# The opening of a two-block transformer and recurrence kernel: the first norm's parameters and the first weight unit are loaded in pieces of their own, and the first weight products stand ahead of the low-rank ones

## The chip, the cores and the metric

The kernel runs on one core of one Trainium2 chip. A core has a matrix engine (TensorE, PE in the profile; its weight loads are PEld), a vector engine (VectorE, DVE), an activation engine (ScalarE, ACT), a general engine (GpSimd, POOL), and SyncE (SP), which here only issues DMA transfers. The metric is the time on the device in microseconds, lower is better.

## The reference

The input is one sequence of 256 positions with 1024 features. Two blocks of two layers each follow one another: a gated linear attention mixer, an attention mixer with rotary positions, each followed by a feed-forward network with a short convolution, then a gated recurrence, a short-convolution mixer, and a last norm. All in float32. Only the beginning matters here:

```
h = rmsnorm(x, norm_mix[0])            # x * rsqrt(mean(x*x) + 1e-6) * weight
proj = h @ w_in
q, k, v, g, r = jnp.split(proj, ...)   # q, k: 512 columns, v, g: 1024, r: 32
r_f, r_b = jnp.split(r, 2, axis=-1)    # the low-rank input of the gates
log_decay = log_sigmoid(r_dir @ w_up + b_up) / 16
```

## The kernel before, in words

**Numbers in two parts.** Each float32 operand of a weight product is split into a high part, which the matrix engine reads in its fast format, and a low part, the difference. A product is three: high by high, high by low, and low by high. For the weights ACT makes the high part (`w_hi`) and DVE the low part (`w_lo`). For the normed input the parts are `h_hi` and `h_lo`, which both lie in the buffer `hh`.

**The stream.** All large weights come from one array, `stream`, in units of 128 by 2048 float32 (1 MB), in the order of their use. SP loads unit u into one of three buffers (`raw`). ACT's `split(u)` writes `w_hi` and adds one to the semaphore `hi_split`. DVE's `split(u)` writes `w_lo`, adds one to `lo_split`, and so frees the raw buffer for unit u + 3. Units 0 and 1 are the columns of q.

**The opening.** There is no scheduler and no loop here; each engine runs a list written by hand, and semaphores join the lists. The 256 positions are two tiles (t = 0, 1) of 128 rows. The order of events is as follows.

- SP issues x (two tiles), then all channel parameters `par` (128 by 548), the low-rank weights `wr`, three raw units, and three copies of the gate weights `gup_raw`. `par` and `wr` count on one semaphore, `consts_loaded`.
- ACT squares x and sums it (`sums`, two halves of 512 columns for each tile). POOL makes 1 / root of the mean from it (`rms_of_x`: the lines 436, 443, 445). DVE multiplies x by it in two halves (`normed`, line 994).
- PE transposes the result, tile by tile, in two groups of four (`turn`, line 1678). Before that it runs 29 transposes of a constant (`WARM`, line 1823), whose results nobody reads.
- The norm's weight is multiplied in as the transposed tile is read from PSUM: by DVE for the first four blocks of tile 0 and for all of tile 1 (`front`, line 1000, semaphore `h_front`), by ACT for the other four of tile 0 (`turned0`, line 524, semaphore `h_hi_ready`). DVE then makes `h_lo` in eight steps (`low`, line 1015), the low part of `wr` (line 1097), and the low parts of units 0 and 1 (line 964).
- PE begins with `rank(0, 0)` (8 products of `wr_hi` and `h_hi`, line 1833), then `product(U_Q, ..)` for unit 0 (16 of high by high, 16 of high by low, line 1844), `rank(0, 1)` and `rank(1, 0)`, the 16 of low by high of unit 0, the 48 of unit 1, the gate products (line 1865), and the units of k (`wide`, line 1764).

POOL issues two more loads on its own queue after the two `rms_of_x` steps: `row` (640 KB written) and `rope` (256 KB).

In PE's list the wait `hi_split` >= 1 stands ahead of the first product of unit 0, and the wait for `wr_hi_ready` ahead of the first rank product.

Of the kernel before, what the change touches and what calls it, by code (L numbers as in the profile page):

```python
# [10 lines left out]
D = 1024  # L11
S = 256
T = S // P
KC = D // P
EPS = 1e-6
# [13 lines left out]
UNIT = 2048  # L29
RAW = 3  # L30
# [106 lines left out]
WARM = 29  # L137
N_CONSTS = 2
# [11 lines left out]
SUMS = {"mix0": 0, "gla": 4, "ffn0": 6, "mix1": 10, "ffn1": 14, "lru": 18, "sc": 22, "final": 26}  # L150
# [23 lines left out]
def two_block_kernel(nc, x_in, stream, par_in, row_in, wr_in, gup_in, gatew_in, rope_in, out):  # L174
# [4 lines left out]
    with ctx:  # L179
        def sem(name):  # L180
            return ctx.enter_context(nc.semaphore(name))
# [85 lines left out]
        consts_loaded, gatew_loaded = sem("consts_loaded"), sem("gatew_loaded")  # L267
# [67 lines left out]
        def copies(a):  # L335

            return a[:, :, :].rearrange("p k (c n) -> p k c n", c=COPIES)
# [21 lines left out]
        def _(sp):  # L359
# [8 lines left out]
            sp.dma_start(par[:, :], par_in).then_inc(consts_loaded, 16)  # L368
            sp.dma_start(wr[:, :, :], wr_in.rearrange("p (c n) -> p c n", c=KC)).then_inc(consts_loaded, 16)
            for u in range(RAW):  # L370
                load(u)
# [36 lines left out]
        def _(pool):  # L408
# [24 lines left out]
            def rms_of_x(name):  # L433
                for t in range(T):
                    pool.wait_ge(sumsq, SUMS[name] + 2 * t + 1)
                    part = nc.gpsimd.tensor_scalar(half_mean[:, t:t + 1], stat[:, 2 * t:2 * t + 1], EPS, None, ALU.add)
                    if name in ROOTS:
                        part.then_inc(half_ready, 1)
                        continue
                    own.mark(part)  # L440
                    own.wait()
                    pool.wait_ge(sumsq, SUMS[name] + 2 * t + 2)
                    own.mark(nc.gpsimd.tensor_tensor(mean[:, t:t + 1], stat[:, 2 * t + 1:2 * t + 2], half_mean[:, t:t + 1], ALU.add))
                    own.wait()
                    nc.gpsimd.tensor_tensor(rstd[:, t:t + 1], mean[:, t:t + 1], power[:, t:t + 1], ALU.pow).then_inc(rms_ready, 1)
# [36 lines left out]
        def _(act):  # L482
# [81 lines left out]
            for t in range(T):  # L564
                act.wait_ge(x_loaded[t], 16)
                sums(t, "mix0")
# [3 lines left out]
            turned0("mix0")  # L570
            split(0)
            split(1)

            own.mark(nc.scalar.activation(lam_p[:, :], par[:, C_LAM:C_LAM + LRU_HEADS], ACT.Abs))
# [382 lines left out]
        def _(dve):  # L957
# [128 lines left out]
            for t in range(T):  # L1086
                dve.wait_ge(x_loaded[t], 16)
                for half in range(2):
                    normed("mix0", t, half)
                if t == 0:  # L1090
                    dve.wait_ge(consts_loaded, 16 * N_CONSTS)
                    front("mix0", 0)
            for b in range(2):
# [4 lines left out]
                                    copies(wr_hi).bitcast(f32), ALU.subtract).then_inc(wr_lo_ready, 1)  # L1098
            split(0)
# [24 lines left out]
            evicted(1)  # L1124
            for d in range(2):
                for b in range(2):
                    dve.wait_ge(z_abs, 2 * d + b + 1)
                    for k in range(2):
                        h = 2 * b + k
                        c = C_GB + GLA_HEADS * d + h  # L1130
                        last = nc.vector.tensor_scalar(la[:, d, h, :], z_of(d, h), par[:, c:c + 1], 0.0, ALU.add, ALU.min)
                        own.mark(last) if k == 0 else last.then_inc(z_read, 1)
# [517 lines left out]
        def _(pe):  # L1650
# [175 lines left out]
            pe.wait_ge(wr_hi_ready, 1)  # L1826
# [10 lines left out]
            def product(u, b, a, c):  # L1837

                for kc in range(KC):
                    if (u, c) == (U_Q, 1):  # L1840
                        has_low("mix0", kc)
# [5 lines left out]

            rank(0, 0)
            pe.wait_ge(hi_split, U_Q + 1)
            product(U_Q, GEN["q"] % 4, 0, 0)  # L1850
# [468 lines left out]
```

## Time and profile before

| | us |
|---|---|
| median of 3 runs | 873.67 (872.7 to 874.02) |
| the profiled execution, its own time | 872.12 |
| its span | 870.1 |
| PE busy in the span | 855.0 (98%) |
| DVE busy | 676.7 (78%) |
| ACT busy | 547.6 (63%) |
| POOL busy | 27.2 (3%) |

The span is the time from the first to the last recorded instruction. Around it lie 2.02 us that the profile does not show. The matrix engine is busy nearly all the time. The change is in the first 20 us of the list, and after it everything is issued in the same order as before.

### The profile page before, as it was taken

To read this page: it belongs to the slowest core of one execution; us is meant where nothing else is said; L and a number is where in the kernel's file an instruction comes from. 1 tells how busy PE (TensorE), PEld (TensorE's weight loads), DVE (VectorE), ACT (ScalarE), POOL (GpSimd) and SP (SyncE) were. 2 spreads that over 40 slices of the span, in tenths; PEclk is the share of its full clock that TensorE was granted. 3 is DMA by queue.
4 is the path that set the end of the run, shared out by engine and by line. 5 is a ranking of instruction groups with operands and counts; after the bars stand their busy time and mean duration, and the time that the engine had idled before them with its cause. 6 is when DMAs were issued, how large, how long until landed. Compare 5 with 4: busy or idle time off the path is not lost.

```text
span 870.1 us, 13406 instructions
## 1 busy us (share of the span) xinstructions
PE 855.0 (98%) x4881; PEld 748.3 (86%) x4881; DVE 676.7 (78%) x966; ACT 547.6 (63%) x750; POOL 27.2 (3%) x48
## 2 busy tenths in 40 slices
PE   8999999999999999999999999999999999999996
PEld 8978789888888888889888888989899788888885
DVE  6898767887877798868787886787887877776764
ACT  5855557656656575576666656568998775555533
POOL 2000100000000041010000000000000000000000
PEclk9999999999999999999999999999999999999998
DMA  8553543665555444226656555435364045645511
GB/s 323 194 197 141 194 145 122 221 220 211 193 199 188 145 161 178 98 98 218 242 194 224 192 199 206 145 145 194 128 234 172 0 153 236 240 173 189 207 59 49
DMA packets 22444, 152.81 MB, mean 176 GB/s; under 512 B 2528, under 2 KB 2656, under 8 KB 5120
## 3 DMA queue, kind: packets, MB, share of 16 engines
q1 hardware_dynamic: 22032, 149.71, 47.4%
q0 software_dynamic: 368, 2.49, 0.8%
q8 instruction: 30, 0.49, 0.2%
q14 instruction: 14, 0.11, 0.0%
HBM read 151.14 MB, written 1.05 MB: 175 GB/s over the span
## 4 chain that ended last, share of the span: by engine, by line
PE 83%; DVE 7%; ACT 2%; DMA 1%; issue 1%; POOLq 0%; POOL 0%; SPq 0%; ACTq 0%; DVEq 0%
PE acc L1777 28%; PE ring L1711 24%; PE ring L1715 12%; PE ring L1764 7%; PE acc L1996 3%; DVE w_lo L964 2%; PE ring L1978 1%; PE ring L1726 1%; DMA raw<-in_stream_dram 1%; DVE hh L1028 1%; PE ring L2036 1%; PE ring L2154 1%; ACT w_hi L491 1%; PE acc L1678 1%; PE acc L1791 0%
## 5 line engine op out<-in xcount | busy, mean ns | idle before, releaser
L964 DVE TENSOR_TENSOR w_lo<-raw,w_hi 128x2048 fp32r<-128x2048 f32 (+1 forms) x145 | 318.0, 2197 | 5.7 <-ACT w_hi L491 5.6
L491 ACT ACTIVATE w_hi<-raw 128x2048 fp32r<-128x2048 f32 (+1 forms) x146 | 266.9, 1840 | 53.3 <-DMA raw<-in_stream_dram 50.0
L1711 PE MATMUL ring<-hh,w_hi 128*128 128x512 f32 x944 | 235.7, 392 | 0.8 <-DVE usum L1079 0.8
L1711 PEld LDWEIGHTS ring<-hh,w_hi 128*128 128x128 f32 x944 | 171.4, 189 | 32.8 <-issue 1.0
L1715 PEld LDWEIGHTS ring<-hh,w_lo 128*128 128x128 f32 x944 | 128.8, 190 | 9.2
L1715 PE MATMUL ring<-hh,w_lo 128*128 128x256 f32 x944 | 131.6, 282 | 0.0
L1777 PE MATMUL acc<-w_hi,a_hi 128*128 128x512 f32 x264 | 103.8, 393 | 1.0 <-DVE a_lo L1304 0.9
L1777 PE MATMUL acc<-w_lo,a_hi 128*128 128x512 f32 x264 | 103.1, 391 | 0.0
L1777 PE MATMUL acc<-w_hi,a_lo 128*128 128x512 f32 x264 | 102.7, 389 | 0.0
L1079 DVE TENSOR_TENSOR usum<-ring,usum 128x512 f32<-128x512 f32 x65 | 44.7, 688 | 63.8 <-ACT usum L496 63.6
L1764 PE MATMUL ring<-hh,w_hi 128*128 128x256 f32 x480 | 87.7, 285 | 0.8 <-DVE gg L1543 0.8
L1274 DVE SCALAR_TENSOR_TENSOR cacc<-usum,par,cacc 128x255 f32<-128x255 f32 x168 | 73.8, 480 | 16.1 <-ACT cacc L648 10.9
L1777 PE MATMUL acc<-w_hi,hh 128*128 128x512 f32 x256 | 84.3, 398 | 1.2 <-DVE hh L1000 0.8
L1764 PEld LDWEIGHTS ring<-hh,w_hi 128*128 128x128 f32 x480 | 75.3, 192 | 1.6 <-issue 1.1
L496 ACT ACTIVATE usum<-ring 128x512 f32<-128x512 f32 x65 | 38.1, 587 | 53.8 <-PE ring L1715 52.3
L1764 PE MATMUL ring<-hh,w_lo 128*128 128x256 f32 x240 | 67.9, 283 | 0.0
L1777 PEld LDWEIGHTS acc<-w_hi,a_hi 128*128 128x128 f32 x264 | 49.7, 188 | 11.2 <-DVE a_lo L1304 1.1
L1777 PEld LDWEIGHTS acc<-w_hi,a_lo 128*128 128x128 f32 x264 | 49.6, 188 | 10.6
L1777 PEld LDWEIGHTS acc<-w_hi,hh 128*128 128x128 f32 x256 | 48.1, 188 | 11.6 <-DVE hh L1000 1.0
L1777 PEld LDWEIGHTS acc<-w_lo,a_hi 128*128 128x128 f32 x264 | 49.7, 188 | 9.0
L1777 PE MATMUL acc<-w_lo,hh 128*128 128x512 f32 x128 | 49.9, 390 | 0.0
L648 ACT ACTIVATE cacc<-usum,par 128x256 f32<-128x256 f32 x84 | 45.5, 590 | 6.9 <-DVE usum L1079 6.9
(242 smaller groups left out, 958.0 us busy)
## 6 DMA issues: line engine op xcount, KB each, us to landing
raw<-in_stream_dram SPq DMA_DIRECT2D x134, 1024.0 KB, 4.8
raw<-in_stream_dram SPq DMA_DIRECT2D x12, 512.0 KB, 3.8
gatew<-in_gatew_dram POOLq DMA_DIRECT2D x1, 1536.0 KB, 7.1
x<-in_x_dram SPq DMA_DIRECT2D x2, 512.0 KB, 3.7
out_dram<-xn SPq DMA_DIRECT2D x2, 512.0 KB, 2.6
row<-in_row_dram POOLq DMA_DIRECT2D x1, 640.0 KB, 9.0
gup_raw<-in_gup_dram SPq DMA_DIRECT2D x3, 128.0 KB, 13.6
par<-in_par_dram SPq DMA_DIRECT2D x1, 274.0 KB, 4.5
```

The costliest lines, as they stand in the source:

```text
L491: nc.scalar.activation(w_hi[:, u % RING, 0:n], raw[:, u % RAW, 0:n], ACT.Copy).then_inc(hi_split, 1)
L496: nc.scalar.activation(usum[:, k, :, :], ring[:, 2 * k:2 * k + 2, S:2 * S], ACT.Copy).then_inc(cross_ready, 1)
L648: last = nc.scalar.activation(cacc[:, k, half, :], ring[:, 2, half * S:(half + 1) * S] if alone else usum[:, k, half, :], ACT.Identity, sc ...
L964: nc.vector.tensor_tensor(w_lo[:, u % RING, 0:n], raw[:, u % RAW, 0:n], w_hi[:, u % RING, 0:n].bitcast(f32), ALU.subtract).then_inc(lo_spl ...
L1028: last = nc.vector.scalar_tensor_tensor(out=h_lo[:, kc, part], in0=turned_at(name, t, kc), scalar=par[:, c:c + 1], in1=h_hi[:, kc, part].b ...
L1079: nc.vector.tensor_tensor(usum[:, k, :, :], ring[:, 2 * k:2 * k + 2, 0:S], usum[:, k, :, :], ALU.add).then_inc(summed, 1)
L1274: last = nc.vector.scalar_tensor_tensor(out=cacc[:, k, half, out_at], in0=at, scalar=par[:, bass.ds(c, 1)], in1=cacc[:, k, half, out_at], ...
L1711: nc.tensor.matmul(ring[:, 2 * k + f, :], w_hi[:, u % RING, lo:lo + P], hh[:, kc, :, :], start=kc == 0, stop=False, skip_group_check=True)
L1715: last = nc.tensor.matmul(ring[:, 2 * k + f, 0:S], w_lo[:, u % RING, lo:lo + P], h_hi[:, kc, :], start=False, stop=kc == KC - 1, skip_grou ...
L1764: last = nc.tensor.matmul(ring[:, b, f * S:(f + 1) * S], w_parts[a][:, slot, lo:lo + P], h_parts[c][:, kc, :], start=kc == 0 and n == 0, s ...
L1777: last = nc.tensor.matmul(acc[:, t, half * 512:(half + 1) * 512], lhs(a, kc, t), w_parts[c][:, slot, j * D + half * 512:j * D + (half + 1) ...
L1996: last = nc.tensor.matmul(acc[:, t, half * 512:(half + 1) * 512], of_h(a, kc, t), w_parts[c][:, (U_AQ + n) % RING, j * D + half * 512:j * ...
```

## The change

Five things are done.

1. **Loads.** The eight columns of `par` that hold the first norm's weight come alone (semaphore `gamma_loaded`), directly behind x. Unit 0 follows in two halves of 128 by 1024 (`raw_front` and `raw_loaded[0]`). Then come `wr`, unit 1, the other 540 columns of `par` (`par_loaded`), unit 2 and the gate weights.
2. **Sums.** For the first norm ACT squares a tile in one instruction of 1024 columns, where there were two of 512. POOL makes the mean in one step instead of two. The numbering of the sums (`SUMS`) follows.
3. **ACT's order.** `turned0` comes first, then the high part of unit 0 in two halves (semaphores `hi_front` and `hi_split`), then `wr_hi`, which stood ahead of both, and then unit 1.
4. **PE's order.** The 16 high by high products of unit 0 come ahead of `rank(0, 0)`, with a wait for each half of `w_hi`.
5. **Warm-up.** `WARM` is 27 instead of 29.

```diff
-            sp.dma_start(par[:, :], par_in).then_inc(consts_loaded, 16)
+            sp.dma_start(par[:, 0:KC], par_in[:, 0:KC]).then_inc(gamma_loaded, 16)
+            half = UNIT // 2
+            sp.dma_start(raw[:, 0, 0:half], stream[0, :, 0:half]).then_inc(raw_front, 16)
+            sp.dma_start(raw[:, 0, half:UNIT], stream[0, :, half:UNIT]).then_inc(raw_loaded[0], 16)
             sp.dma_start(wr[:, :, :], wr_in.rearrange("p (c n) -> p c n", c=KC)).then_inc(consts_loaded, 16)
-            for u in range(RAW):
-                load(u)
+            load(1)
+            sp.dma_start(par[:, KC:N_PAR], par_in[:, KC:N_PAR]).then_inc(par_loaded, 16)
+            load(2)
...
                 for t in range(T):
-                    pool.wait_ge(sumsq, SUMS[name] + 2 * t + 1)
-                    part = nc.gpsimd.tensor_scalar(half_mean[:, t:t + 1], stat[:, 2 * t:2 * t + 1], EPS, None, ALU.add)
...
-                    own.mark(part)
-                    own.wait()
-                    pool.wait_ge(sumsq, SUMS[name] + 2 * t + 2)
-                    own.mark(nc.gpsimd.tensor_tensor(mean[:, t:t + 1], stat[:, 2 * t + 1:2 * t + 2], half_mean[:, t:t + 1], ALU.add))
+                    pool.wait_ge(sumsq, SUMS[name] + t + 1)
+                    own.mark(nc.gpsimd.tensor_scalar(mean[:, t:t + 1], stat[:, 2 * t + 1:2 * t + 2], EPS, None, ALU.add))
                     own.wait()
...
             for t in range(T):
                 act.wait_ge(x_loaded[t], 16)
-                sums(t, "mix0")
+                nc.scalar.activation(xn[:, t, :], x[:, t, :], ACT.Square, scale=D ** -0.5,
+                                     accum_out=stat[:, 2 * t + 1:2 * t + 2]).then_inc(sumsq, 1)
+            act.wait_ge(gamma_loaded, 16)
+            turned0("mix0")
+            for part in range(2):
+                at = slice(part * UNIT // 2, (part + 1) * UNIT // 2)
+                act.wait_ge(*((raw_front, 16), (raw_loaded[0], 16))[part])
+                nc.scalar.activation(w_hi[:, 0, at], raw[:, 0, at], ACT.Copy).then_inc((hi_front, hi_split)[part], 1)
             act.wait_ge(consts_loaded, 16 * N_CONSTS)
...
-            turned0("mix0")
-            split(0)
             split(1)
 
+            act.wait_ge(par_loaded, 16)
...
             def product(u, b, a, c):
 
                 for kc in range(KC):
+                    if (u, a, c) == (U_Q, 0, 0):
+                        if kc % 4 == 0:
+                            pe.wait_ge(*((hi_front, 1), (hi_split, 1))[kc // 4])
+                        for t in range(T):
+                            has_high("mix0", t, kc)
...
+            product(U_Q, GEN["q"] % 4, 0, 0)
+            pe.wait_ge(wr_hi_ready, 1)
             rank(0, 0)
-            pe.wait_ge(hi_split, U_Q + 1)
-            product(U_Q, GEN["q"] % 4, 0, 0)
             product(U_Q, GEN["q"] % 4, 0, 1)
```

On PE, at the end of the transposes in the opening, the list of before reads as follows; `ring<-hh,wr_hi` is a rank product, `ring<-hh,w_hi` one of unit 0.

```order
L1678 MATMUL acc<-ident,xn 128x128 x3
L1833 MATMUL ring<-hh,wr_hi 96x256 [waits h_front,wr_hi_ready]
L1833 MATMUL ring<-hh,wr_hi 96x256 x3
L1833 MATMUL ring<-hh,wr_hi 96x256 [waits h_front,h_hi_ready]
L1833 MATMUL ring<-hh,wr_hi 96x256 x3
L1844 MATMUL ring<-hh,w_hi 128x256 [waits hi_split]
L1844 MATMUL ring<-hh,w_hi 128x256 x15
L1844 MATMUL ring<-hh,w_hi 128x256 [waits h_lo_ready]
```

At the same place on PE the changed list reads as follows, with the lines numbered by the changed file (1688 is `turn`, 1842 the rank product, 1858 the product of a unit).

```order
L1688 MATMUL acc<-ident,xn 128x128 x3
L1858 MATMUL ring<-hh,w_hi 128x256 [waits h_front,hi_front]
L1858 MATMUL ring<-hh,w_hi 128x256 x7
L1858 MATMUL ring<-hh,w_hi 128x256 [waits h_front,h_hi_ready,hi_split]
L1858 MATMUL ring<-hh,w_hi 128x256 x7
L1842 MATMUL ring<-hh,wr_hi 96x256 [waits h_front,wr_hi_ready]
L1842 MATMUL ring<-hh,wr_hi 96x256 x3
L1842 MATMUL ring<-hh,wr_hi 96x256 [waits h_front,h_hi_ready]
L1842 MATMUL ring<-hh,wr_hi 96x256 x3
L1858 MATMUL ring<-hh,w_hi 128x256 [waits h_lo_ready]
```

The sixteen products of unit 0 moved ahead of the eight rank products, and the wait for all of `w_hi` became one for each half.

On ACT, from the start of its list, before:

```order
L506 ACTIVATE xn,stat<-x 128x512 [waits x_loaded0]
L506 ACTIVATE xn,stat<-x 128x512
L506 ACTIVATE xn,stat<-x 128x512 [waits x_loaded1]
L506 ACTIVATE xn,stat<-x 128x512
L568 ACTIVATE wr_hi<-wr 128x768 [waits consts_loaded]
L524 ACTIVATE hh<-acc,par 128x128 [waits x_turned]
L524 ACTIVATE hh<-acc,par 128x128 x3
L491 ACTIVATE w_hi<-raw 128x2048 [waits raw_loaded0]
L491 ACTIVATE w_hi<-raw 128x2048 [waits raw_loaded1]
L574 ACTIVATE lam_p<-par 128x12
```

And changed, the same piece of ACT's list (568 squares, 526 is `turned0`, 575 and 493 split a unit, 577 is `wr_hi`):

```order
L568 ACTIVATE xn,stat<-x 128x1024 [waits x_loaded0]
L568 ACTIVATE xn,stat<-x 128x1024 [waits x_loaded1]
L526 ACTIVATE hh<-acc,par 128x128 [waits x_turned,gamma_loaded]
L526 ACTIVATE hh<-acc,par 128x128 x3
L575 ACTIVATE w_hi<-raw 128x1024 [waits raw_front]
L575 ACTIVATE w_hi<-raw 128x1024 [waits raw_loaded0]
L577 ACTIVATE wr_hi<-wr 128x768 [waits consts_loaded]
L493 ACTIVATE w_hi<-raw 128x2048 [waits raw_loaded1]
L582 ACTIVATE lam_p<-par 128x12 [waits par_loaded]
```

Two squares became one in each tile, `wr_hi` moved behind the first unit, and that unit is split in halves.

## Rows read from the trace of the kernel before

**Rows 1.** Page, busy time by engine.

```profile
PE 855.0 (98%) x4881; PEld 748.3 (86%) x4881; DVE 676.7 (78%) x966; ACT 547.6 (63%) x750; POOL 27.2 (3%) x48
```

**Rows 2.** Busy time in stretches (us, busy and count by engine, clock, DMA share, GB/s).

```profile
8.26:9.07 0.81, 0.00 (x1) 0.00 (x1) 0.81 (x3) 0.77 (x4) 0.80 (x2) 1.00 1.04 425
...
11.72:17.43 5.71, 5.71 (x50) 5.64 (x48) 5.71 (x10) 3.02 (x4) 0.00 (x0) 1.00 1.01 352
17.43:32.12 14.69, 14.69 (x124) 14.69 (x123) 13.03 (x16) 10.57 (x14) 0.00 (x0) 1.00 0.76 289
60.50:860.00 799.50, 795.07 (x4504) 694.68 (x4505) 620.61 (x869) 506.36 (x695) 20.52 (x27) 1.00 0.47 171
```

**Rows 3.** Timeline, first norm: start, duration, engine, line, operation, count, [idle before, releaser].

```profile
1.72 0.42 SPq L368 DMA_DIRECT2D par<-in_par_dram  x1
...
5.31 0.19 ACT L506 ACTIVATION_READ_ACCUMULATOR xn<-x 128x1 f32 x1
...
5.65 0.19 POOL L443 TENSOR_TENSOR mean<-stat,half_mean 128x1 f32<-128x1 f32 x1 [0.46 <-ACT xn L506]
5.92 0.58 POOL L445 TENSOR_TENSOR rstd<-mean,power 128x1 f32<-128x1 f32 x1
...
6.62 0.88 DVE L994 TENSOR_SCALAR xn<-x,rstd 128x512 f32<-128x512 f32 x2 [6.62 <-POOL rstd L445]
...
7.12 0.85 ACT L568 ACTIVATE wr_hi<-wr 128x768 fp32r<-128x768 f32 x1 [0.38 <-DMA wr<-in_wr_dram]
...
7.93 0.69 DVE L1000 TENSOR_TENSOR hh<-acc,par 128x512 fp32r<-128x512 f32 x1 [0.42 <-PE acc L1678]
...
8.30 1.14 ACT L524 ACTIVATE hh<-acc,par 128x128 fp32r<-128x128 f32 x4 [0.33 <-PE acc L1678]
```

**Rows 4.** Forms of two ACT groups: duration ns min/median/max.

```profile
L506 ACT ACTIVATE xn<-x x4: 613/621/630, 4.2 to 6.0; 128x512 f32<-128x512 f32 x4
...
L614 ACT ACTIVATE v<-acc x2: 1017/1021/1025, 60.4 to 61.4; 128x1024 f32<-128x1024 f32 x2
```

**Rows 5.** Timeline, from the second tile to the first low products.

```profile
9.59 1.92 ACT L491 ACTIVATE w_hi<-raw 128x2048 fp32r<-128x2048 f32 x1 [0.15 <-DMA raw<-in_stream_dram]
9.76 1.29 DVE L1000 TENSOR_TENSOR hh<-acc,par 128x512 fp32r<-128x512 f32 x2 [0.26 <-PE acc L1678]
10.60 1.28 PE L1833 MATMUL ring<-hh,wr_hi 128*96 128x256 f32 x8 [0.38 <-DVE hh L1000]
...
11.08 3.23 DVE L1015 SCALAR_TENSOR_TENSOR hh<-acc,par,hh 128x256 fp32r<-128x256 f32 x8
...
11.72 3.99 PE L1844 MATMUL ring<-hh,w_hi 128*128 128x256 f32 x32
...
15.09 4.49 DVE L964 TENSOR_TENSOR w_lo<-raw,w_hi 128x2048 fp32r<-128x2048 f32 x2
...
16.49 1.10 PE L1833 MATMUL ring<-hh,wr_lo 128*96 128x256 f32 x8
...
17.43 2.19 PE L1844 MATMUL ring<-hh,w_lo 128*128 128x256 f32 x16
```

**Rows 6.** Timeline, where PE and DVE meet again.

```profile
16.64 1.92 ACT L491 ACTIVATE w_hi<-raw 128x2048 fp32r<-128x2048 f32 x1 [2.29 <-DMA raw<-in_stream_dram]
...
32.12 0.69 DVE L1119 COPY kT<-ring 128x512 f32<-128x512 f32 x1 [1.54 <-PE ring L1764]
```

**Rows 7.** Chain of waits that ended last (start, duration, piece), around 60 us.

```profile
60.35 0.11 DVE qt L1200
...
60.50 0.49 PE ring L1881 x2
```

**Rows 8.** DMA issues of the channel parameters: size, us from issue to landing.

```profile
par<-in_par_dram SPq DMA_DIRECT2D x1, 274.0 KB, 4.5
```

**Rows 9.** Timeline, the warm-up transposes, early and late.

```profile
1.43 1.97 PE L1823 MATMUL ring<-ident 128*128 128x128 f32 x8 [1.43 <-POOL ident L412]
...
4.68 2.04 PE L1823 MATMUL ring<-ident 128*128 128x128 f32 x14
```

More of the change, by code:

```diff
@@ L136 @@
 LO = KC
-WARM = 29
-N_CONSTS = 2
+WARM = 27
+N_CONSTS = 1
 COPIES = 3
@@ L148 @@
 ROOTS = ["ffn0", "mix1", "ffn1", "lru", "sc", "final"]
-SUMS = {"mix0": 0, "gla": 4, "ffn0": 6, "mix1": 10, "ffn1": 14, "lru": 18, "sc": 22, "final": 26}
+SUMS = {"mix0": 0, "gla": 2, "ffn0": 4, "mix1": 8, "ffn1": 12, "lru": 16, "sc": 20, "final": 24}
 class Chain:
@@ L266, in two_block_kernel @@
         x_loaded = [sem(f"x_loaded{t}") for t in range(T)]
-        consts_loaded, gatew_loaded = sem("consts_loaded"), sem("gatew_loaded")
+        gamma_loaded, consts_loaded, gatew_loaded = sem("gamma_loaded"), sem("consts_loaded"), sem("gatew_loaded")
+        par_loaded, raw_front, hi_front = sem("par_loaded"), sem("raw_front"), sem("hi_front")
         rows_loaded = sem("rows_loaded")
@@ L434, in rms_of_x @@
                 for t in range(T):
-                    pool.wait_ge(sumsq, SUMS[name] + 2 * t + 1)
-                    part = nc.gpsimd.tensor_scalar(half_mean[:, t:t + 1], stat[:, 2 * t:2 * t + 1], EPS, None, ALU.add)
                     if name in ROOTS:
-                        part.then_inc(half_ready, 1)
+                        pool.wait_ge(sumsq, SUMS[name] + 2 * t + 1)
+                        nc.gpsimd.tensor_scalar(half_mean[:, t:t + 1], stat[:, 2 * t:2 * t + 1], EPS, None, ALU.add).then_inc(half_ready, 1)
                         continue
-                    own.mark(part)
-                    own.wait()
-                    pool.wait_ge(sumsq, SUMS[name] + 2 * t + 2)
-                    own.mark(nc.gpsimd.tensor_tensor(mean[:, t:t + 1], stat[:, 2 * t + 1:2 * t + 2], half_mean[:, t:t + 1], ALU.add))
+                    pool.wait_ge(sumsq, SUMS[name] + t + 1)
+                    own.mark(nc.gpsimd.tensor_scalar(mean[:, t:t + 1], stat[:, 2 * t + 1:2 * t + 2], EPS, None, ALU.add))
                     own.wait()
@@ L1090, in _ @@
                 if t == 0:
-                    dve.wait_ge(consts_loaded, 16 * N_CONSTS)
+                    dve.wait_ge(gamma_loaded, 16)
                     front("mix0", 0)
@@ L1098, in _ @@
                                     copies(wr_hi).bitcast(f32), ALU.subtract).then_inc(wr_lo_ready, 1)
+            dve.wait_ge(hi_front, 1)
             split(0)
@@ L1124, in _ @@
             evicted(1)
+            dve.wait_ge(par_loaded, 16)
             for d in range(2):
@@ L1825, in _ @@
                 turn("mix0", t)
-            pe.wait_ge(wr_hi_ready, 1)
             def rank(a, c):
```

## The prediction

> **What bounds the kernel now.** I read the page first. PE is busy for 855.0 of 870.1 us [rows 1], and in the 799.5 us behind 60.50 for 795.07 [rows 2]. Behind the opening the kernel is one long row of matmuls in an order that the change leaves alone, so the change is worth the time by which the opening hands over earlier, and no more. The second view, the stretches, shows where PE's row begins: from 11.72 to 32.12 PE has no idle time at all [rows 2]. The third, the timeline of the first 20 us, shows what stands ahead of it. POOL's `rstd` of tile 0 ends at 6.50 and DVE starts on it at 6.62, the transposes and the `hh` steps of DVE follow, and PE's first rank product starts at 10.60, released by DVE [rows 3, 5]. The reader should see that DVE and PE hand this chain to each other, while ACT waits for transfers: 0.38 us for `wr`, 0.15 us for unit 0 [rows 3, 5], 2.29 us for unit 2 [rows 6].
>
> DVE matters again later. At 32.12 it copies `kT`, released by PE after 1.54 us of idle time [rows 6]. The chain of waits then lies on DVE up to 60.46, and from 60.50 on PE [rows 7]. So what PE gains before 32.12 goes through that copy into DVE's row, and through DVE into the long row of PE.
>
> **The change part by part.**
>
> *One square in place of two, one mean step in place of two.* Before, ACT's second read of the accumulator starts at 5.31, ends at 5.50, and POOL's `mean` starts at 5.65, `rstd` at 5.92 [rows 3]. Two squares of 512 take 0.62 us each, 1.24 together. One operation of 128x1024 on ACT takes 1.02 [rows 4]; that one reads another source and computes a copy, so its length is a stand-in. Against it, the slope from the 512 form (0.62) to the 2048 form (1.92, rows 5) gives 0.62 + 512 x 0.85 ns = 1.05. The saving is 0.22 or 0.19, and the accumulator's first read lay beside the second square. POOL's remaining operation gains or loses a few hundredths. I take 0.17 for the time at which DVE starts on tile 0, with 0.10 and 0.25 as ends. If x itself arrived later the gain would be gone, but its two transfers stand first in SP's list in both versions.
>
> *Tile 1.* Its `rstd` isn't what DVE waits for. DVE goes from `front` of tile 0 (7.93 to 8.62) straight to tile 1, and then waits only 0.26 for transposes [rows 3, 5]. The whole DVE row up to the last `h_lo` step moves by 0.17.
>
> *Parameters in a piece of their own.* Before, `par` is issued at 1.72 and landed 4.5 later, at 6.2 [rows 3, 8]. DVE's first use is at 7.93, released by PE and not by the transfer [rows 3]. Loading eight columns first makes them earlier by what 274 KB take, which nobody waits for. This part is worth nothing. The cover is 7.93 - 0.17 - 6.2 = 1.5 us, and beyond it each us late costs a us. The trace has no transfer with pieces as small as these, 32 bytes for a partition. The nearest row is `par` itself, whose landing at 6.2 I take as the later end.
>
> On small pieces the Trainium skill speaks against the change: "DMA: Bandwidth & Descriptors", Specifications, says that a transfer reaches line rate only from 512 bytes, and that below it the engine reads, modifies and writes. By line rate alone that costs nothing that can be seen on 4 KB, so the sum would be the same by row and by page, and no row here shows the rule itself.
>
> *Unit 0 in halves.* ACT's `hh` steps end at 9.44 and the split of unit 0 starts at 9.59, released by the transfer, ends at 11.51, and PE's product starts at 11.72 [rows 3, 5]. In the new order the steps end at 9.27. The 274 KB of `par` and the 128 KB of `wr` no longer lie ahead of unit 0, so by then it has landed: 402 KB are about 1 us at the 425 GB/s of that stretch [rows 2], which puts the second half at 8.6. The first half (1.02 to 1.05) is ready at 10.3, the second at 11.3. With the 0.21 from the end of a split to PE's start, as now, PE could begin at 10.5 and needs the second half 8 products later, at 11.5.
>
> *Unit 0's products ahead of rank.* PE needs the first four blocks of `hh` of tile 1 for either: DVE's step ends at 9.76 + 0.69 = 10.45, and PE starts at 10.60 [rows 5]. That becomes 10.43. So PE starts at about 10.5, where rank started at 10.60. Now rank takes from 10.60 to 11.72, 1.12 us; the eight rank products at 16.49 take 17.43 - 16.49 = 0.94 [rows 5]. The 0.18 between are two short waits, for the second half of `hh` and for `w_hi`, and the eight products of unit 0 (0.95) bridge them. PE's row could so be 0.1 + 0.18 = 0.28 earlier. `wr_hi`, moved behind unit 0 on ACT, ends at 11.3 + 0.85 = 12.15, and PE asks for it at 10.5 + 1.9 = 12.4: covered by 0.25. Without that cover a late `wr_hi` costs its lateness. ACT then splits unit 1 from 12.15 to 14.1, and PE needs it only when the 16 low products of unit 0 are done, at 19.4.
>
> *What is late next.* PE's first product with `w_lo` starts at 17.43. The last rank product is issued until 17.43, and DVE's first low part ends at 15.09 + 2.28 = 17.37 [rows 5]. The two arrive together. In the new version PE arrives at 17.15, and DVE, whose row is busy without a gap from 10.9 (8 steps, `wr_lo`, the split), at 17.20. PE so waits for DVE, and of the 0.28 only DVE's 0.17 are left. That is the term that sets the sum.
>
> *From there to 60.5.* Both engines are shifted by the same 0.17. ACT's unit 2 stays where it is, since the bytes ahead of it are the same in sum (16.64 with its wait of 2.29, rows 6), so its high part ends at 18.56; DVE is busy with units 0 and 1 until 19.58 [rows 5], so that this costs nothing up to 1 us. POOL's two loads are issued 0.17 earlier. The remainder of `par` now stands between units 1 and 2 and is first needed by ACT behind unit 1, at 14.1. By the sum of bytes it comes 0.65 us (274 KB at 425 GB/s) behind unit 1 and 2.5 ahead of unit 2's end at 16.6, so at 14.1 at the latest. Two fewer warm-up transposes save at most nothing: they end at 6.72 now, before DVE's first output at 7.1 (6.62 and half of 0.88) [rows 3, 9].
>
> **Sum.** 872.12 - 0.17 = 871.95 for the profiled execution, or 0.2 us less, 0.02%. The ends are 0.0 (a late `w_hi` or `wr_hi` takes the gain) and 0.3 (the low part doesn't bind). The profiled execution stands 1.55 below the median of the three runs, 873.67. By the median the forecast is 873.5; by the mean of all four figures (873.1) it is 872.9. I take 873.2. The three runs spread by 1.3 us, so 0.2% (1.75 us) is about what a measurement can tell, and the effect is a tenth of it.
>
> **The rivals.**
>
> *The gain is swallowed.* The halves end late on ACT, or the unit's transfer in two pieces of 4 KB for a partition is slower than one, so that PE starts at 10.6 to 10.8 and is back in step at 17.43. Against it stands the cover computed above. It gives 872.1 by the profile, 873.4 by my middle: the same verdict. Chance 12%.
>
> *PE's clock falls in the opening, and the kernel is slower.* PE is idle for about 0.4 us before the first transposes (6.72 to 7.1), 0.81 between the tiles [rows 2] and 0.38 before the rank products [rows 5]. The change takes 2 transposes from the warm-up, each about 0.15 [rows 9], so the first gap grows to 0.5 or 0.6. The granted clock is 1.00 there, the 2.4 GHz level. The early warm-up transposes take 1.97 / 8 = 0.25 us each, the late ones 2.04 / 14 = 0.15 [rows 9], so a slow pace does exist. If PE fell back to it from 10.5 for as long as it lasted at first (1.43 to 4.7, 3.3 us), work done at half speed would lose 1.6 us, and the sum would be +1.5: 874.7. It decides if PE stays slow for over 4 us. For it speaks only the longer gap, and against it that gaps of 0.81 leave the clock at 1.00. Chance 5%.
>
> The Trainium skill, "TensorE: Matmul & The Clock Gate", Part 1, says that the clock falls to half after enough idleness and comes back only after sustained work. The gaps of this trace, which leave the clock up, bear out that short ones are harmless.
>
> *The first parameters land after DVE needs them, slower.* With the other small pieces this would delay everything one for one. It decides (over 1.75 + 0.17 late) only if they land after 9.7, which is 3.5 later than the whole of `par` does today. Chance 2%.
>
> *More is gained than the opening can show.* The opening would have to give 1.75 us. From ACT's first square at 4.2 [rows 4] to PE's first product are 6.4 us, and no row shows a gap of that size on the path. What is left is the setting of the runs. Chance 9%, with 871.5 as its time.
>
> **How the numbers follow.** The forecast (0.1 to 0.3 gained) has 72%, the swallowed gain 12%, the two slow ones 7%, the large gain 9%. With the runs' spread, faster by over 0.2% has 10%, within it 83%, slower 7%. The range from 871.6 to 874.8 is the middle plus and minus 1.6, that is the spread of the runs on each side and the clock rival's 874.7; outside it are most of the large gain and the late parameters.
>
> **What would show it.** In the changed profile DVE's first `xn` should start at 6.45 instead of 6.62, the first product of unit 0 at 10.4 to 10.6, and the first one with `w_lo` at 17.2 to 17.3, with DVE's low part as its releaser. DVE's `kT` copy should start at 31.9 to 32.0, PE's products at line 1881 of before at 60.3. Wrong would be a first product after 10.8, a clock below 1.00 before 20 us, or a difference between 17.4 and 60.5 other than that before it.

## The result and the profile after

The changed kernel is slower, by about a quarter of a per cent: 875.88 us median (9 runs, 874.55 to 876.84) against 872.74 us (9 runs, 871.51 to 874.73), ratio 1.0026 with a 95% interval of 1.0015 to 1.0036. The forecast was 873.2, range 871.6 to 874.8. The profiled execution took 876.44 us, 4.3 us over that of before, with a span of 874.7 (before: 870.1). Of all runs below only one, of the kernel before beside e13 and e14, lies far from the rest, at 4844 us: the ratios leave it out, and without it the median there is 873.03 and not 873.15.

Here are the lines of the changed kernel's page that answer to [rows 1].

```profile
PE 856.1 (98%) x4879; PEld 749.0 (86%) x4879; DVE 676.9 (77%) x966; ACT 547.1 (63%) x747; POOL 27.0 (3%) x46
PEclk9999999999999999999999999999999999999999
```

PE was busy 1.1 us longer (855.0 before), in a span that is 4.6 us longer, so most of the loss is time in which PE waits. This is the timeline of the changed kernel's opening, to be laid beside [rows 3, 5, 6].

```profile
6.46 0.88 DVE L1002 TENSOR_SCALAR xn<-x,rstd 128x512 f32<-128x512 f32 x2 [6.46 <-POOL rstd L447]
...
9.21 2.02 ACT L575 ACTIVATE w_hi<-raw 128x1024 fp32r<-128x1024 f32 x2
...
10.45 2.15 PE L1858 MATMUL ring<-hh,w_hi 128*128 128x256 f32 x16 [0.44 <-DVE hh L1008]
...
17.28 1.97 PEld L1858 LDWEIGHTS ring<-hh,w_lo 128*128 128x128 f32 x16 [0.16 <-DVE w_lo L972]
...
20.20 1.91 ACT L493 ACTIVATE w_hi<-raw 128x2048 fp32r<-128x2048 f32 x1 [4.38 <-DMA raw<-in_stream_dram]
22.02 1.04 ACT L587 ACTIVATE gup<-gup_raw 96x1024 fp32r<-96x1024 f32 x1
...
23.10 1.22 DVE L1118 TENSOR_TENSOR gup<-gup_raw,gup 32x1024 fp32r<-32x1024 f32 x1 [2.89 <-ACT gup L587]
...
33.21 0.68 DVE L1128 COPY kT<-ring 128x512 f32<-128x512 f32 x1
```

Up to 17.28 DVE and PE are as forecast: DVE at 6.46, PE's first product at 10.45, and the first with `w_lo` at 17.28, where PE waits for DVE. ACT is not. It splits unit 1 at 13.04 instead of 12.15 and reads the rest of `par` at 15.37 instead of 14.1, each time after waiting for the transfer, which PE doesn't feel yet. Then ACT waits 4.38 us for unit 2, which it splits at 20.20 instead of 16.64. The gate step stands behind that split in ACT's list, and DVE idles 2.89 us for it. DVE's row is 2.71 us late (20.39 to 23.10). The 1.54 us for which DVE used to wait for PE at `kT` [rows 6] swallow a part, and 33.21 - 32.12 = 1.09 stay. PE's step that started at 60.50 [rows 7] comes 1.10 us later:

```profile
61.60 0.49 PE L1895 MATMUL ring<-qd,ki 128*128 128x128 f32 x2
```

Why unit 2 is late is seen in the stretches: first the changed kernel (the last columns are the clock, the DMA share and GB/s).

```profile
4.00:5.00 1.00, 1.00 (x9) 1.00 (x8) 0.00 (x0) 0.78 (x1) 0.00 (x0) 1.00 0.88 302
5.00:6.00 1.00, 1.00 (x11) 0.88 (x9) 0.00 (x0) 0.67 (x3) 0.46 (x2) 1.00 0.70 140
6.00:7.00 1.00, 0.12 (x2) 0.00 (x0) 0.54 (x2) 0.85 (x2) 0.41 (x2) 1.00 0.73 197
...
17.00:18.00 1.00, 1.00 (x9) 0.84 (x9) 1.00 (x2) 0.00 (x0) 0.00 (x0) 1.00 1.03 238
18.00:19.00 1.00, 1.00 (x11) 1.00 (x10) 1.00 (x1) 0.00 (x0) 0.00 (x0) 1.00 0.80 201
19.00:20.00 1.00, 1.00 (x10) 1.00 (x10) 0.96 (x3) 0.00 (x0) 0.00 (x0) 1.00 1.18 279
20.00:21.00 1.00, 1.00 (x11) 1.00 (x10) 0.21 (x1) 0.80 (x1) 0.00 (x0) 1.00 1.00 209
```

And stretches of the kernel before at the same places.

```profile
5.00:6.00 1.00, 1.00 (x9) 1.00 (x8) 0.00 (x0) 1.00 (x4) 0.46 (x3) 1.00 1.02 368
6.00:7.00 1.00, 0.73 (x7) 0.49 (x5) 0.38 (x1) 0.74 (x4) 0.83 (x3) 1.00 0.99 391
...
16.00:17.00 1.00, 1.00 (x11) 1.00 (x10) 1.00 (x1) 0.36 (x1) 0.00 (x0) 1.00 1.03 266
17.00:18.00 1.00, 1.00 (x10) 0.93 (x9) 1.00 (x2) 1.00 (x1) 0.00 (x0) 1.00 0.62 148
18.00:19.00 1.00, 1.00 (x11) 1.00 (x10) 1.00 (x1) 0.76 (x2) 0.00 (x0) 1.00 0.28 37
```

There are two effects. From 5 to 7 us the rate falls to 140 and 197 GB/s where it was 368 and 391. That is a hole of some 0.42 MB, about 1 us. From 17 to 21 us the rate is near 230 GB/s at a full DMA share: unit 2 and the gate weights (three transfers of 32 pieces of 4 KB, each into 32 partitions) lie beside each other. Before, ACT could split unit 2 at 16.64, and what then still ran, at 266, 148 and 37 GB/s, delayed no unit.

A second loss lies far behind the change. In the changed kernel's waits between 396 and 425 us, and in its stretches there, one reads:

```profile
PE acc L1787 <- DVE a_lo L1314: 2.2, 1, 2.2
```

```profile
415.00:418.00 3.00, 0.97 (x4) 0.79 (x5) 2.30 (x3) 2.38 (x3) 0.00 (x0) 0.94 0.57 183
418.00:421.00 3.00, 3.00 (x9) 2.33 (x8) 3.00 (x3) 1.65 (x3) 0.00 (x0) 0.50 0.57 194
```

At the start of the second feed-forward layer PE waits 2.2 us (before: 0.9), and behind that wait the granted clock is 0.50 (the 1.2 GHz level) for 3 us. There the shift to the kernel before grows from 1.1 to 3.9 us, of which 1.3 are the wait and 1.5 the clock.

### The profile page after: what moved, and what is told of

Same layout as the page of the kernel before. It is cut to its first block, busy times and chain, and to the rows that moved or that the text cites. A ratio compares the mean times of both kernels' runs of the same rounds, so it can differ in the third digit from the quotient of the medians.

```text
span 874.7 us, 13402 instructions
## 1 busy us (share of the span) xinstructions
PE 856.1 (98%) x4879; PEld 749.0 (86%) x4879; DVE 676.9 (77%) x966; ACT 547.1 (63%) x747; POOL 27.0 (3%) x46
## 4 chain that ended last, share of the span: by engine, by line
PE 82%; DVE 7%; ACT 2%; DMA 2%; issue 1%; POOLq 0%; POOL 0%; SPq 0%; ACTq 0%; DVEq 0%
PE acc L1787 28%; PE ring L1721 24%; PE ring L1725 12%; PE ring L1774 7%; DVE w_lo L972 3%; PE acc L2010 3%; DMA raw<-in_stream_dram 2%; PE ring L1992 1%; PE ring L1736 1%; DVE hh L1036 1%; ACT w_hi L493 1%; PE ring L2050 1%; PE ring L2168 1%; PE acc L1688 1%; PE acc L1801 0%
## 6 DMA issues: line engine op xcount, KB each, us to landing
gup_raw<-in_gup_dram SPq DMA_DIRECT2D x3, 128.0 KB, 14.1
```

## The experiments

The columns of the table are: the start of ACT's split of unit 2, the start of DVE's gate step, how much later than before (60.50) PE reaches the step of [rows 7], and the median with the number of runs beside that of the kernel before on the same chip. Chips differ (the kernel before has medians of 871.96 to 873.15 on them), so medians are compared within a line or with lines of the same chip. The first three columns come from one profiled execution each.

| | unit 2 | DVE gate | at 60.50 | median (runs) | before there | chip | ratio (95%) |
|---|---|---|---|---|---|---|---|
| before | 16.64 | 20.39 | 0 | 872.74 (9) | | | |
| changed | 20.20 | 23.10 | +1.10 | 875.88 (9) | 872.74 | | 1.0026 (1.0015 to 1.0036) |
| e1 engines' order alone | 16.81 | 20.18 | -0.19 | 871.26 (11) | 873.06 | A | 0.9980 (0.9971 to 0.9989) |
| e2 transfers alone | 19.41 | 22.31 | +2.23 | 876.76 (5) | 873.06 | A | 1.0044 (1.0030 to 1.0057) |
| e3 par whole | 18.29 | 21.18 | +0.06 | 872.40 (11) | 873.06 | A | 0.9996 (0.9986 to 1.0007) |
| e4 unit 0 whole | 16.69 | 20.48 | -0.06 | 872.48 (11) | 873.06 | A | 0.9994 (0.9985 to 1.0003) |
| e5 before, gatew late | 15.57 | 20.48 | +0.09 | 871.11 (12) | 872.84 | B | 0.9979 (0.9968 to 0.9990) |
| e6 changed, gatew late | 21.39 | 24.28 | +2.28 | 873.04 (12) | 872.84 | B | 1.0002 (0.9991 to 1.0012) |
| e7 order alone, gatew late | 19.74 | 22.70 | +4.07 | 871.11 (12) | 872.84 | B | 0.9981 (0.9969 to 0.9992) |
| e8 three small, moved | 18.96 | 21.85 | +0.55 | 877.49 (5) | 872.84 | B | 1.0050 (1.0033 to 1.0067) |
| e9 as e7, 29 warm-ups | 19.70 | 22.60 | +2.92 | 870.87 (11) | 871.96 | C | 0.9986 (0.9975 to 0.9998) |
| e10 halves alone | 18.09 | 21.72 | +0.06 | 872.54 (10) | 871.96 | C | 0.9999 (0.9987 to 1.0010) |
| e11 three small again | 17.36 | 20.33 | +0.23 | 872.50 (10) | 871.96 | C | 1.0015 (0.9998 to 1.0031) |
| e12 first piece on ACT's queue | 18.51 | 21.41 | +0.10 | 872.23 (10) | 871.96 | C | 0.9999 (0.9988 to 1.0011) |
| e13 gates behind unit 2 | 18.13 | 22.57 | +1.61 | 874.46 (11) | 873.15 | D | 1.0018 (1.0009 to 1.0027) |
| e14 squares, gatew late | 15.96 | 20.23 | -0.16 | 870.90 (11) | 873.15 | D | 0.9976 (0.9967 to 0.9985) |

**e1: the new order on the engines, the transfers of before.**

```diff
 (changed kernel)
-            sp.dma_start(par[:, 0:KC], par_in[:, 0:KC]).then_inc(gamma_loaded, 16)
-            (unit 0 in halves, wr, unit 1, the rest of par, unit 2)
+            sp.dma_start(par[:, :], par_in).then_inc(gamma_loaded, 16)
+            (wr, units 0, 1 and 2 whole)
```

> All of the change on ACT, POOL, DVE and PE, but the transfers of before: par whole, wr, three whole units. Theory T (the transfers): unit 2's high part starts on ACT at 16.6 to 16.9 as before (20.2 in the changed kernel), DVE's gup step at 20.2 (23.1), DVE's kT copy at 31.9 to 32.0 (33.2), and the time is that of before less about 0.2 us, ratio 0.9995 to 1.0000. Rival O (the new order on the engines is what costs): unit 2 is again split at 20 or later and the ratio is near the changed kernel's 1.0026.

The timeline of e1 on ACT:

```profile
9.45 2.01 ACT L571 ACTIVATE w_hi<-raw 128x1024 fp32r<-128x1024 f32 x2 [0.17 <-DMA raw<-in_stream_dram]
...
16.81 1.92 ACT L489 ACTIVATE w_hi<-raw 128x2048 fp32r<-128x2048 f32 x1 [2.48 <-DMA raw<-in_stream_dram]
```

Unit 2 is back at 16.81, DVE's gate step at 20.18 and `kT` at 31.91. PE's step of 60.50 comes 0.19 earlier, where the forecast's sum had 0.17. The new order on the engines costs nothing, so the transfers are the cause of the loss. The time fell by 1.8 us, though, and the opening explains a tenth of that.

**e2: the new transfers, the engines' order of before.**

> The transfers of the change, and the engines' orders of before (the waits are adapted). Theory T: unit 2's high part starts at 20 or later, kT at 33.2 to 33.4, about 1.2 to 1.4 us later than before at 60 us, ratio 1.0015 to 1.003. Rival O: unit 2 at 16.6, ratio 1.000.

The transfers alone cost 3.7 us, and unit 2 is late again (19.41), as theory T has it. The path of this loss is another, though. ACT still asks for `wr` first, which now comes behind unit 0, so unit 0 is split late and PE starts its products at 13.93 instead of 11.72:

```profile
10.20 0.84 ACT L573 ACTIVATE wr_hi<-wr 128x768 fp32r<-128x768 f32 x1 [2.90 <-DMA wr<-in_wr_dram]
...
13.93 4.09 PE L1853 MATMUL ring<-hh,w_hi 128*128 128x256 f32 x32 [1.09 <-ACT w_hi L496]
```

Those 2.21 us are the whole +2.23 at 60.50, and DVE waits for PE at `kT` (34.34). So the new order on ACT and PE repairs a wait that the new transfers bring, and e2 is no second measure of what a late unit 2 costs. Whether its loss is larger than the changed kernel's is not shown, since the intervals overlap.

**e3 and e4: one of the two new cuts undone in the changed kernel, the first par piece (e3) or the halves of unit 0 (e4).**

```diff
 (e3)
-            sp.dma_start(par[:, 0:KC], par_in[:, 0:KC]).then_inc(gamma_loaded, 16)
+            sp.dma_start(par[:, :], par_in).then_inc(gamma_loaded, 16)
 (e4)
-            (raw_front and raw_loaded[0], a half each)
+            load(0)
```

> The changed kernel with par in one transfer again, at the place of the first eight columns; unit 0 stays in halves and ahead of wr. Theory T1 (the 32-byte pieces of the eight columns open the hole of 5 to 7 us, where the rate falls from 390 to 140 to 200 GB/s): no hole, unit 2 split at 16.6 to 17.2, time of before less 0.1. Rival T2 (the halves of unit 0 disorder the engines): unit 2 still after 19, time as the changed kernel's.

> The changed kernel with unit 0 in one transfer again; the eight columns stay in a piece of their own. Theory T1 (32-byte pieces): the hole stays and unit 2 is split after 19, time as the changed kernel's. Rival T2 (halves): unit 2 at 16.6 to 17.2. PE's first product of unit 0 stays at 10.4 to 10.7 in both.

Neither theory held alone. With the halves alone (e3) unit 2 comes 1.65 us late and with the small piece alone (e4) on time, and neither loses anything at 60.50. Both together cost 3.6 us at unit 2. The rate from 5 to 6 us shows the same, first in e3, then in e4:

```profile
5.00:6.00 1.00, 1.00 (x7) 1.00 (x6) 0.00 (x0) 0.94 (x3) 0.55 (x2) 1.00 0.77 224
...
5.00:6.00 1.00, 1.00 (x11) 1.00 (x10) 0.00 (x0) 0.25 (x2) 0.58 (x2) 1.00 1.00 300
```

In the six profiles that have both cuts in SP's queue (three of the changed kernel, e2, e6 and e13) it is 67 to 140 GB/s, and in all others at least 224.

Against e1, on the same chip and with the same order on the engines, the medians of e3 and e4 are 1.1 and 1.2 us higher, of which the openings (+0.06 and -0.06 against -0.19) explain a quarter of a us at most. Where the rest lies is not shown.

The small piece is not free: in e4 the second tile of x is squared only at 6.21, where it was 5.41.

```profile
6.21 1.06 ACT L566 ACTIVATE xn<-x 128x1024 f32<-128x1024 f32 x1 [0.96 <-DMA x<-in_x_dram]
```

POOL's `rstd` for it ended at 8.34, just when DVE was through with the step before, so this was covered with nothing to spare. e3's profiled execution shows a wait of 2.6 us at 414 and a fallen clock behind it, and at 874.76 it was one of two in eleven over 873.4.

**e10 and e12: the halves in their old place (e1 with unit 0 cut), and the small piece issued from ACT's queue.**

```diff
 (e12, changed kernel)
-            sp.dma_start(par[:, 0:KC], par_in[:, 0:KC]).then_inc(gamma_loaded, 16)
+            act.dma_start(par[:, 0:KC], par_in[:, 0:KC]).then_inc(gamma_loaded, 16)
```

> e1 with unit 0 in two transfers of 4 KB per partition, in the place where it stands before (behind par and wr). Theory T2 (one more transfer, and shorter pieces, in front of the stream open the hole): the rate falls under 300 GB/s somewhere between 5 and 8 us, unit 2 is split at 17.5 to 18.5, the time is e1's plus 0 to 0.5. Rival (in e3 it was wr behind unit 0 that did it): unit 2 at 16.8.

> The changed kernel with the transfer of the eight columns issued from ACT's queue instead of SP's. Theory Q (a small transfer costs because it takes a turn in SP's queue): the second tile of x is squared at 5.4 or earlier (5.7 in the changed kernel), unit 2 is split at about 18.3 as in e3, and the time is e3's, 872.4. Rival P (its 128 pieces cost wherever they are issued): unit 2 after 19.5, time as the changed kernel's.

The halves alone, wherever they stand, put unit 2 at 18.1 to 18.5, with a dent of 224 to 268 GB/s somewhere between 5 and 8 us. By ratio e10 stands 1.7 us over e1, where I expected 0.5 at most, and its opening (+0.06) doesn't explain that. In e12 the same 128 pieces, on ACT's queue, add nothing to the halves at unit 2 (18.51, and +0.10 at 60.50). Theory Q held there, on one profile and a median 0.3 us over before, but not in its first sign: the second tile of x is squared at 5.76, where I expected 5.4. ACT issues the piece at 0.81 and not at 1.72, so that it lies beside x: the rate from 2 to 3 us is 173 GB/s (332 in the changed kernel), and the first square starts at 4.47 instead of 4.22. So e12 changes the time of the piece along with its queue. What the runs show is that the hole needs both the 4 KB transfer in SP's queue and the cut unit behind it. How the two act together no run shows.

**e8 and e11: e1 with three more small transfers behind x, 4 KB each.** In e8 they go to a new buffer, in e11 into the row buffer.

> e1 with three more transfers of 128 pieces of 32 bytes (12 KB in all, into a buffer that nobody reads) behind x. Theory S (a transfer holds SP's queue for a time of its own however few its bytes): a hole of about 2 us or more in the rate between 4.5 and 8 us, par, wr and the units late by as much, PE's first product at 11 or later, unit 2 at 18 or later, and 1 to 3 us more than e1. Rival B (only bytes count, 0.03 us for 12 KB): all as in e1.

> e8 again, with the three transfers of 32-byte pieces written into a place of the row buffer, so that no other buffer moves (in e8 all buffers behind the new one moved by 128 bytes, and PE's products from a_hi took 397 instead of 393 ns). Theory S: opening as in e8, unit 0 at 10.2, unit 2 at about 19, and 0.5 to 2 us more than e1 in all, not 6. Rival: 6 us more again.

Both theories missed in size. Unit 0 is 0.4 to 0.75 us late and unit 2 is 0.55 (e11) to 2.15 (e8), for 12 KB, which at the rate of the stream are 0.03 us. So bytes alone don't price a transfer. There is no hole under 340 GB/s, though: with whole units behind them, small transfers cost tenths. Most of e8's 6.2 us over e1 are of another kind: its new buffer moved all later ones by 128 bytes. Three groups of products that read `a_hi` and `a_lo` took 397, 395 and 394 ns, where e1's took 393, 389 and 391, over 264 each: 3.4 us, at a granted clock of 1.00. In e11, where no buffer moved, they took 393, 389 and 391 again. The opening adds 0.7 us, and some 2 us of e8 stay unexplained. e11 has three of its ten runs at 875.3 to 877.4, which its profiled one (871.32) doesn't explain either.

**e13: the changed kernel, with the gate weights issued only when unit 2 has landed.**

```diff
             load(2)
+            sp.wait_ge(raw_loaded[2], 16)
             for c in range(COPIES):
```

> The changed kernel, but SP issues the three gate-weight transfers only when unit 2 has landed. In the changed kernel the rate from 16 to 21 us is 200 to 280 GB/s at a full DMA share, while unit 2 and the gate weights share the engines; unit 2 lands at 20 to 22. Theory O (overlap: the 32-partition gate transfers slow unit 2 down, and the hole at 5 to 7 us only sets it 1.2 us back): unit 2 is split at 17.5 to 18.5, the gate weights at 20.5 to 22, DVE's gup step at 21.5 to 23, and the opening's loss falls from about 2 to 0.5 to 1.2 us; the ratio to before is 1.000 to 1.001. Rival H (the hole alone makes unit 2 late): unit 2 after 19.5, gate weights at 22.5 or later, loss 2 to 3 us, ratio 1.002 to 1.004.

Unit 2 is split at 18.13, with the hole of 5 to 7 us in place (91 and 233 GB/s). So, by one profile each, 2 us of unit 2's lateness are the overlap with the gate weights, and about 1.5 the hole and halves. The loss did not fall to the 0.5 to 1.2 us expected (1.61). Unit 3 stands behind the gate weights in SP's list and is now split at 25.85:

```profile
25.85 1.92 ACT L494 ACTIVATE w_hi<-raw 128x2048 fp32r<-128x2048 f32 x1 [3.31 <-DMA raw<-in_stream_dram]
```

In the four profiles with the changed transfers as they are (three of the changed kernel, and e6) `kT` stands 10.11 us behind DVE's gate step each time, so the gate step sets it. Here it is 11.17 behind, at 33.74, since DVE now waits for the late unit 3:

```profile
27.80 2.29 DVE L973 TENSOR_TENSOR w_lo<-raw,w_hi 128x2048 fp32r<-128x2048 f32 x1 [0.96 <-ACT w_hi L494]
```

**e5, e6 and e7: the kernels before, changed and e1, each with the recurrence's gate weights (1.5 MB, issued by POOL at 390.6) held back into the middle of the layer.**

```diff
+            pool.wait_ge(hi_split, U_FFN[1] + 16)
             pool.dma_start(gatew[:, :, :], gatew_in...)
```

> The kernel before, with one transfer moved: the 1.5 MB gate weights of the recurrence (gatew), which POOL issues at 390.6 as the second feed-forward layer starts, wait until unit 75 has been split, in the middle of that layer. Theory G (the stall of PE at 414 us, 0.6 to 2.6 us in the five profiles, comes from gatew's packets lying between those of the stream): the wait of PE for a_lo falls to 0.5 or less, the time by 0.4 to 1.5 us, and no clock fall at 417. Rival: the stall stays at 0.6 to 2.6, it is the stream's own latency, and the time is that of before.

> The changed kernel with the same move of gatew. Theory G: the stall and the fall of the clock at 417 are gone, and only the opening's loss stays: e5's median plus 1.1 to 1.4 us, and the two clusters of the changed kernel's runs (874.6 and 876.4) become one. Rival: the changed kernel still stands 2.5 to 3 us above before, and the clock still falls.

> The new order on the engines, the transfers of before, and gatew late. If e1's 1.8 us over before are the opening's 0.2 and the rest fewer stalls at 414, then e7 stands 0.2 us below e5. If e1 has a gain of another kind, e7 stands 1 us or more below e5.

Theory G held in the spread of the runs and in the wait, and the gain is larger than the 0.4 to 1.5 us expected (1.73). PE's waits of 0.6 us or more in e5 have no `a_lo` among them. This is its list from the third row on (the first two are of the start):

```profile
PE ring L1727 <- DVE hh L1029: 0.8, 1, 0.8
PE ring L1765 <- DVE gg L1544: 0.8, 1, 0.8
PE acc L1778 <- DVE hh L1001: 0.8, 1, 0.8
PE ring L1712 <- DVE usum L1080: 0.6, 1, 0.6
```

One profile without the wait would not show it, since the wait is missing from some profiles of the other kernels too. But e5's runs lie within 1.0 us (870.78 to 871.78), where the kernel before spreads over 5. e6 minus e5 is 1.93 us, where 1.1 to 1.4 were expected. With the stall gone that is the price of the opening, close to the +2.28 of e6's profile, and e6's runs still spread over 2.7 us. e7 has the same median as e5, and nine of its twelve runs lie at 870.4 to 871.4. The profiled one took 874.96, and its stretches show the rival that I had given 5%: the granted clock falls in the opening.

```profile
8.00:11.40 3.40, 1.09 (x8) 0.86 (x8) 2.98 (x6) 1.45 (x5) 1.23 (x2) 0.99 1.02 428
11.40:18.20 6.80, 6.00 (x28) 6.01 (x29) 6.80 (x11) 4.65 (x6) 0.00 (x0) 0.50 0.96 335
```

PE was busy for 1.09 of 3.40 us, since unit 0 came late (split at 11.09), and then for 6.8 us ran at 0.50. Why unit 0 was late with the transfers of before stays open.

**e9 and e14: e7 with 29 warm-up transposes, and e5 with nothing of the change but one square per tile and one mean step.**

> e7 with 29 warm-up transposes instead of 27. e7's profile shows a granted clock of 0.5 from 11.4 to 18.2 us. If the two transposes less cause such falls, e9 has none among its runs: all within 870.3 to 871.5, where e7 has three of twelve at 873.0 to 875.0. If the falls come from the wait for unit 0's transfer (1.9 us in that profile), e9 has such runs too. The typical run is 870.9 in both.

> e5 with only the one square per tile and the one mean step of the change; PE's, ACT's and SP's orders are those of before. Theory: DVE's first xn at 6.46 instead of 6.62 and 0.2 us less than e5 in the typical run (870.9 where e5 has 871.1 on the same chip), and none of the runs at 872.9 to 875 that e7 and e9 have, because PE begins with rank products and doesn't wait for unit 0. Rival (those runs come with any order): 2 or 3 of 12 runs over 872.5.

e9 has three of eleven runs at 872.3 to 873.8, and its profile again has the late unit 0 and a clock of 0.50 from 13.3 to 16.6. Two transposes more don't prevent it.

```profile
13.30:16.60 3.30, 3.30 (x17) 3.30 (x17) 3.30 (x6) 2.54 (x4) 0.00 (x0) 0.50 1.02 359
```

e14 has no run over 871.64, and its opening is 0.16 us early. It beats both kernels: 870.90 us, ratio 0.9976 (0.9967 to 0.9985). That is the late gate weights' gain. Beside e5's 0.9979 the squares' own 0.16 us can't be seen in the times.

**Two more profiles of each kernel.**

> The changed kernel once more, for its profile. Theory L (the opening's loss is in every run, the stall at 414 us and the fall of the clock behind it are in some): PE's first product of unit 4 (the wait at 54.6 us of before) 0.9 to 2.4 us later than before's; a wait of PE for a_lo at 415 to 420 us anywhere from 0.5 to 2.6; where it is over 2, a clock of 0.5 for 3.4 us behind it and a time of about 876.5, otherwise about 874.6.

> The kernel before once more. Theory L: opening within 0.2 us of the first profile, the wait at 414 again anywhere from 0.5 to 2.6, and a time over 873.4 only with a clock of 0.5 behind it. Rival: the wait at 414 is always 0.9 in the kernel before, so that the change makes it longer.

> The changed kernel once more. As for the first repeat: opening 0.9 to 2.4 us later than before's, the wait at 415 to 420 from 0.5 to 2.6 us, and a fallen clock only where that wait is over 2.

> The kernel before once more. As for the first repeat: opening within 0.2 us of the first profile, the wait at 414 anywhere from 0.5 to 2.6 us by theory L, always 0.9 by the rival.

| | time | at 60.50 | PE's wait for a_lo | clock of 0.50 behind it |
|---|---|---|---|---|
| before (first) | 872.12 | 0 | 0.9 | no |
| b1 | 871.07 | -0.04 | 0.1 at most | no |
| b2 | 874.21 | +0.59 | 1.8 | no |
| changed (first) | 876.44 | +1.10 | 2.2 | yes |
| a1 | 873.71 | +1.99 | 0.3 at most | no |
| a2 | 874.63 | +2.82 | 0.1 at most | no |

Theory L held for what matters. In the changed kernel the rate from 5 to 6 us is 67 and 95 GB/s, and unit 2 is split at 20.55 and 21.94, so the hole comes each time. The opening costs 1.10, 1.99 and 2.82 us in the changed kernel, 1.97 on average, and 0 to 0.59 in the kernel before, 0.18 on average. The difference of 1.8 is e6 minus e5 again. The wait at 414 comes and goes in both kernels. Five details missed: a1 took 873.71 and not about 874.6, b2 took 874.21 without a fallen clock, its opening was 0.59 late and not within 0.2, a2's was 2.82 late and not 2.4 at most, and the wait was under the 0.5 expected in a1, a2 and b1.

b2, e7 and e9 are a warning on single profiles. With the transfers of before, unit 2 was split at 18.48, 19.74 and 19.70 in them, as late as in runs with the new transfers, and the rate from 5 to 6 us was 250 to 260 GB/s. A late unit 2 by itself does not prove the new transfers. A rate of 140 or less there does not occur without them, and the medians of e1, e3 and e4 stand beside it.

## Why the prediction was wrong

The sum's term for the norm was right. I had 0.17, and e14 shows 0.16 and e1 0.19. PE's first product at 10.45, the wait for DVE's low part at 17.28, and the path of a shift over `kT` into 60.50 came as written. So did the reason why the earlier parameters and the bridged waits of PE bring nothing further.

The step that failed is this sentence: "ACT's unit 2 stays where it is, since the bytes ahead of it are the same in sum". The bytes were the same. The list of transfers was not: two more of them, one of 4 KB, and pieces of 4 KB instead of 8. The rate fell from 5 to 7 us (first effect). The later units were late with it, unit 1 too (13.04 instead of 12.15), and the rest of `par`, which I had at 14.1 at the latest, held ACT until 15.37. Unit 2 then met the gate weights at 16 to 21 us (second effect, 2 us by e13). I had noted the cover, "up to 1 us", and unit 2 came 3.6 to 5.3 us late. The rival of swallowed gain named "two pieces of 4 KB" as slower, but followed the lateness to unit 0 alone, and not to the last transfers in the same queue, where all of it adds up. Unit 0 cost next to nothing: in a2 and e6 ACT waited 0.20 us for its second half, and PE's first product with `w_lo` stood at 17.41 instead of 17.28. ACT's list then carried it on, since the gate step stands behind the split of unit 2.

Of the 2.3 us that the ratio 1.0026 means, the opening is 1.8 to 1.9. The rest is within what the stall at 414 and the clock behind it do from run to run in both kernels. That the change makes them likelier is not shown. The 3.1 us between the medians and why e1 stands 1.8 us under before, where e7 and e5 are equal, also stay open. Many profiles of e1 and of the changed kernel would settle that.

The Trainium skill's "DMA: Bandwidth & Descriptors", Specifications, puts pieces under 512 bytes below line rate. As a price that is too small here: even at an eighth of the 425 GB/s of [rows 2], a share that I assume, 4 KB would by my estimate take under 0.1 us, and the hole was 1 us. And the same 32-byte pieces ahead of a whole unit 0 (e4) left unit 2 at 16.69. So what this case shows is no matter of line rate.

The rival of the clock had a price that came out right, with luck. I had 1.6 us for a fall of 3.3 us, and 1.5 was measured at 418 us. But I took the length from the slow warm-up transposes, and the stretch from 1.40 to 3.00 us, where they stand, has a granted clock of 1.00, so they show no fall:

```profile
1.40:3.00 1.60, 1.57 (x8) 1.58 (x9) 0.00 (x0) 0.68 (x1) 1.32 (x5) 1.00 0.71 200
```

In e7 the fall lasted 6.8 us. And it struck in a place that I had not looked at, and in the opening only where unit 0 was late. The Trainium skill's "TensorE: Matmul & The Clock Gate", Part 1, says that idleness brings the clock down. The trace agrees: falls followed waits of 2.2 us (changed) and 2.6 us (e3) and a stretch with PE busy for 1.09 of 3.40 us (e7), and the waits for `a_lo` of 0.6 to 1.8 us were followed by none.

## What to carry to other kernels

When the order or the cutting of transfers in a full queue changes, recompute the landing of the last of them and not only of the one that was moved. Bytes in sum are not enough: here the same bytes in two more transfers came 3.6 to 5.3 us later. Ask which step stands behind a late transfer in an engine's list. A small early piece cost nothing at the last unit in front of a whole unit (e4) or on ACT's queue (e12, where x came 0.25 us later), and was dear on SP's queue in front of a unit that was cut too. The best step found here was elsewhere: a 1.5 MB load moved out of a layer's start is worth 1.7 us (e5, ratio 0.9979), ten times the 0.17 us forecast for the opening. And after a change that costs tenths of a us, one profile is not enough, since the opening of the kernel before alone varied by 0.6 us.

## What the runs showed of the hardware that I had not expected

- Three transfers of 32 pieces of 4 KB, each into 32 partitions (the gate weights), beside a unit of 128 partitions: 201 to 279 GB/s at a DMA share of 0.80 to 1.18 (changed kernel, 17 to 21 us). From 13 to 15 us, without them, it was 425 and 431. That the number of partitions is the reason is not shown.
- A 4 KB transfer in SP's queue ahead of a unit in two halves: 67 to 140 GB/s from 5 to 6 us, in six profiles of six. With one of the two alone it was 224 or more.
- With buffers moved by 128 bytes PE's products from `a_hi` and `a_lo` took 3 to 6 ns longer (393 to 397, 389 to 395, 391 to 394), 3.4 us in all (e8; e11, where nothing moved, has the old times).
- A wait of PE of 2.2 us cost 3.7 us, the wait itself and 1.5 us at the 1.2 GHz level behind it (changed kernel, 415 to 421 us). No fall followed a wait of 1.8 us (b2).
